# Up projection of a hybrid decoder layer: 16 of 22 tile pairs with seven products, in runs of three and four

## The reference, cut to what matters

```python
h2 = _rmsnorm(x, g_ffn)
f = jnp.einsum("btd,df->btf", h2, w_up)
f_gate, f_up = jnp.split(f, [D_FF], axis=-1)
f_conv, new_f = _causal_dwconv(f_gate, buf_f, conv_f_w)
x = x + jnp.einsum("btf,fd->btd", jax.nn.silu(f_conv) * f_up, w_down)
```

## Time and profile before

| | us |
|---|---|
| median of 3 runs | 856.12 (856.05 to 856.14) |
| the profiled execution: its own time | 856.21 |
| its span, first to last instruction | 854.2 |
| PE busy | 840.2 (98%) |
| DVE busy | 665.6 (78%) |
| ACT busy | 407.7 (48%) |
| mean granted clock of TensorE | 0.999 |

### The profile page before, as it was taken

How to read it: one execution, slowest core, us unless ns; L and a number is a source line. 1 busy time by engine, 2 the same in 40 slices (tenths; PEclk the granted TensorE clock), 3 DMA queues, 4 the chain that set the end, 5 groups by cost and what they waited for, 6 DMA issues and landing times.

```text
span 854.2 us, 18315 instructions
## 1 busy us (share of the span) xinstructions
PE 840.2 (98%) x6948; PEld 835.8 (98%) x6948; DVE 665.6 (78%) x983; ACT 407.7 (48%) x733; POOL 128.9 (15%) x98
## 2 busy tenths in 40 slices
PE   8999999999999999999999989999999999999996
PEld 7999999999999999999999979999999999999996
DVE  4899998999999965766579898888888888544343
ACT  7753646364342244762245655454454457332232
POOL 2283837475000000000012200000000000000000
PEclk9999999999999999999999999999999999999999
DMA  9423233432432333218632123333333334353323
GB/s 258 125 85 113 76 98 98 134 100 87 126 104 76 99 110 99 76 49 159 161 100 74 50 81 101 97 94 100 102 97 101 107 92 129 93 133 98 95 75 113
DMA packets 189160, 88.92 MB, mean 104 GB/s; under 512 B 34758, under 2 KB 187644, under 8 KB 189076
## 3 DMA queue, kind: packets, MB, share of 16 engines
q1 hardware_dynamic: 186225, 86.29, 36.0%
q10 hardware_dynamic: 2875, 1.82, 0.8%
HBM read 83.79 MB, written 3.51 MB: 102 GB/s over the span
## 4 chain that ended last, share of the span: by engine, by line
PE 91%; DVE 5%; issue 1%; ACT 1%; DMA 0%; DVEq 0%; SPq 0%; ACTq 0%
PE psum L1715 44%; PE psum L1721 22%; PE psum L1891 8%; PE psum L1919 6%; PE psum L1896 4%; PE psum L1924 3%; PE psum L2032 1%; DVE w_lo L1364 1%; DVE tmp L1474 1%; PE psum L2041 1%; PE psum L1693 1%; PE psum L1758 1%; PE psum L1756 1%; DMA v<-in_x_prompt 0%; PE psum L1765 0%
## 5 line engine op out<-in xcount | busy, mean ns | idle before, releaser
L1715 PE MATMUL psum<-act,w_hi 128*128 128x260 f32 x2600 | 341.1, 282 | 0.0
L1715 PEld LDWEIGHTS psum<-act,w_hi 128*128 128x128 f32 x2600 | 323.0, 188 | 0.0
L1069 DVE TENSOR_TENSOR w_lo<-raw,w_hi 128x1024 fp32r<-128x1024 f32 (+2 forms) x110 | 129.9, 1183 | 77.2 <-ACT w_hi L544 76.7
L1721 PE MATMUL psum<-act,w_lo 128*128 128x260 f32 x1300 | 185.1, 282 | 0.0
L1721 PEld LDWEIGHTS psum<-act,w_lo 128*128 128x128 f32 x1300 | 168.1, 188 | 0.0
L544 ACT ACTIVATE w_hi<-raw 128x1024 fp32r<-128x1024 f32 (+2 forms) x110 | 107.1, 976 | 88.2 <-PE psum L1721 85.7
L512 POOL TENSOR_TENSOR gate_a<-gate_a,prods 128x512 f32<-128x512 f32 x72 | 110.1, 1529 | 79.6 <-ACT prods L629 71.2
L1891 PE MATMUL psum<-act,w_hi 128*128 128x260 f32 x448 | 71.3, 283 | 3.0 <-ACT tmp L891 2.7
L1364 DVE TENSOR_TENSOR w_lo<-raw,w_hi 128x1024 fp32r<-128x1024 f32 x44 | 53.6, 1222 | 24.2 <-ACT w_hi L815 24.2
L1919 PE MATMUL psum<-mid,w_hi 128*128 128x260 f32 x512 | 68.1, 283 | 0.0
L1146 DVE SCALAR_TENSOR_TENSOR psum<-u,cst,psum 128x512 f32<-128x512 f32 x96 | 66.8, 746 | 0.0
(11 more groups left out here) (208 smaller groups left out, 999.6 us busy)
## 6 DMA issues: line engine op xcount, KB each, us to landing
raw<-in_w_in SPq DMA_DIRECT2D x56, 512.0 KB, 3.7
raw<-in_w_up SPq DMA_DIRECT2D x44, 512.0 KB, 3.8
raw<-in_w_down SPq DMA_DIRECT2D x16, 384.0 KB, 3.9
raw<-in_w_down SPq DMA_DIRECT2D x16, 320.0 KB, 3.2
v<-in_x_prompt SPq DMA_DIRECT2D x8, 512.0 KB, 6.3
raw<-in_w_b_out SPq DMA_DIRECT2D x8, 512.0 KB, 3.7
raw<-in_w_a_out SPq DMA_DIRECT2D x8, 512.0 KB, 5.1
raw<-in_w_o SPq DMA_DIRECT2D x8, 512.0 KB, 4.3
```

Source lines behind the costliest of these rows:

```text
L1069: ve.tensor_tensor(w_lo[:, slot, 0:k, :], raw[:, s, 0:k, :], w_hi[:, slot, 0:k, :], ALU.subtract).then_inc(lo_done, 1)
L1715: pe.matmul(a[:, h, :], w_hi[:, s, j, :], rhs(k, part)[:, h * H:(h + 1) * H], start=start and part == 0, stop=False)
L1721: last = pe.matmul(a[:, h, :], w_lo[:, s, j, :], rhs(k, 0)[:, h * H:(h + 1) * H], start=False, stop=stop)
```

## The change

The plain steps are now 0, 4, 8, 13, 17 and 21: six, and 16 steps have seven products, in runs of three (1 to 3, 5 to 7, 14 to 16, 18 to 20) and one of four (9 to 12). The chain's bank comes from a table: in a run of three banks 0, 2, 3, in a run of four banks 0, 1, 2, 3. Since banks 0 and 1 are also those of the plain gate product, two waits come in: P1 of a step whose bank is 0 or 1 waits for `cx_set` of the last plain step (DVE's `plain_gate` has read the gate banks), and a plain gate product waits for `prod_done` of the last step that used them. On ACT `silu(n - 1)` moves behind `up_5(n)` in steps that follow another step with seven, and in step 1; in the other first steps of a run it stays ahead of `up_v`. On DVE `weight_sum_4(n + 1)` moves ahead of `up_22(n)`. `turn_root` goes with the third plain step, now step 8.

```diff
-    PLAIN = tuple(range(0, FT, 3))
+    PLAIN = (0, 4, 8, 13, 17, 21)
...
+        IN_RUN = [n - max(m for m in PLAIN if m <= n) - 1 for n in range(FT)]
+        RUN = [next((m for m in PLAIN if m > n), FT) - max(m for m in PLAIN if m <= n) - 1 for n in range(FT)]
+        BANK_X = [((0, 2, 3) if RUN[n] == 3 else (0, 1, 2, 3))[IN_RUN[n]] if SEVEN[n] else None for n in range(FT)]
...
         def bank_x(n):
-            return psum[:, 2 if TURN[n] else 3, 0:H]
+            return psum[:, BANK_X[n], 0:H]
...
         def last_x(n):
-            return max((m for m in range(n) if SEVEN[m] and TURN[m] == TURN[n]), default=None)
+            return max((m for m in range(n) if BANK_X[m] == BANK_X[n]), default=None)
+
+        def last_in_gate_banks(n):
+            return max(m for m in range(n) if BANK_X[m] in (0, 1))
...
                 hi_open(n + 1)
-                if FOLLOWS[n]:
-                    up_v(n)
+                if not FOLLOWS[n] and n > 1:
                     silu(n - 1)
-                else:
+                up_v(n)
+                up_5(n)
+                if FOLLOWS[n] or n == 1:
                     silu(n - 1)
-                    up_v(n)
-                up_5(n)
...
-                up_22(n)
                 if SEVEN[n + 1]:
                     weight_sum_4(n + 1)
+                up_22(n)
...
                     pe.wait_ge(cx_set, PLAIN[PLAIN.index(n) - 1] + 1)
+                    pe.wait_ge(prod_done, START + 2 * KT + last_in_gate_banks(n) + 1)
                     plain(n, "gate", gate_banks, 1, at_4=lambda: fourth(n - 1))
...
                 if last_x(n) is not None:
                     pe.wait_ge(prod_done, START + 2 * KT + last_x(n) + 1)
+                if BANK_X[n] in (0, 1):
+                    pe.wait_ge(cx_set, max(m for m in PLAIN if m < n) + 1)
                 product("P1", n)
```

More of the change, by code:

```diff
@@ L310, in build @@
         assert PLAIN[0] == 0 and PLAIN[-1] == FT - 1 and SEVEN[1]
+        IN_RUN = [n - max(m for m in PLAIN if m <= n) - 1 for n in range(FT)]
+        RUN = [next((m for m in PLAIN if m > n), FT) - max(m for m in PLAIN if m <= n) - 1 for n in range(FT)]
+        BANK_X = [((0, 2, 3) if RUN[n] == 3 else (0, 1, 2, 3))[IN_RUN[n]] if SEVEN[n] else None for n in range(FT)]
+        assert all(RUN[n] in (3, 4) for n in range(FT) if SEVEN[n])
         def bank_x(n):
-            return psum[:, 2 if TURN[n] else 3, 0:H]
+            return psum[:, BANK_X[n], 0:H]
         def banks_zy(n):
```

## The result

The changed kernel takes 863.87 us, the median of 4 runs (863.71 to 864.04), against 856.12 before (4 runs, 856.05 to 856.14): a ratio of 1.0091, 95% interval 1.0076 to 1.0106. It is 7.75 us slower; 8.0 were forecast. The profiled execution took 863.88 us with a span of 861.8, so the 2.0 us around the span are unchanged. The down projection starts at 727.44 us, where it started at 719.88 before. The first matmul of the up projection starts at 478.44, where it was 478.57. So this stage is 7.69 us longer and what lies ahead of it 0.13 shorter, and nothing behind it changed. PE's busy time fell by 0.4 us and DVE's rose by 9.3.

The account below looks back on a forecast made before the run. PE, 91% of the chain, was taken to bound the kernel through its work and waits. Terms -3.0 + 1.8 + 9.75 + 1.7 - 2.0 = +8.2, taken as +8.0 on 856.21, gave 864.2 us; range 862.4 to 866.6.

Parts of the forecast that it names:

- The matmuls saved: On PE, two plain steps become steps with seven products, 11.57 to 10.06 us each: 3.0 us down.
- P1 of step 1: P1 waits for `cx_set` and starts 5.2 us late; after waits that shrink, step 3 begins 1.8 us later: 1.8 up.
- The clock: Forecast: clock stays at 1.00 behind step 1's wait. Rival (30%): it falls in the 5.2 us idle, +9.1, 865.3 us.
- Middle steps: Steps 2, 6, 10, 11, 15, 19: DVE needs 12.0 us, PE 10.06, so P4 waits for `up_22`; with step 3, 9.75 up.
- the lead of each run: How far `up_22`'s result is ahead of P4 at a run's start: 1.0 us, between 0.9 and 1.5.
- P1 of a run's first step: P1 waits for `plain_gate`: 1.5 us at step 9 behind `turn_root`, 0.2 at step 5; together 1.7 up.
- Waits that go: `silu` behind the copies frees P3 in the last step of a run: 0.7, 0.9 and four times 0.1, 2.0 down.
- The price of a later `silu`: On ACT, moving `silu` behind the copies was put at nothing, as DVE has other work ahead of the product needing it.
- The likeliest case: The forecast as worked out, +8.0 us to 864.2, without a clock fall: 60%, 862.4 to 865.
- not slower: Rival (3%): DVE keeps up in middle steps as its 1.34 us wait for ACT shrinks; -0.5, 855.7 us.

Follow-up runs that it names:

- The experiment that keeps PE busy: The changed kernel with 42 matmuls without use into free bank 2 ahead of P1 of step 1, whose wait stays: 862.43 us.
- the experiment with another bank: The changed kernel with banks 2, 0, 3 in the first run, so that P1 of step 1 has a free bank: 860.15 us.
- orders alone: The kernel before with only the change's two order edits, `silu` on ACT and `weight_sum_4` on DVE; runs of two and old banks stay: 853.05 us.
- POOL: The kernel with banks 2, 0, 3 first and earlier weight sums, plus the third weight-sum pass on POOL and plain steps 0, 3, 9, 15, 21: 855.08 us.
- both repairs: The changed kernel with banks 2, 0, 3 in the first run and `weight_sums(n + 1)` ahead of `lo_3(n)` in middle steps: 853.50 us.
- another bank behind `turn_root`: The changed kernel with banks 2, 0, 1, 3 in the run of four (steps 9 to 12): 863.19 us.

## Why the prediction was right

The sign, the size and the places were right. By the steps of the sum:

- *The matmuls saved*, 3.0 down: 6924 matmuls on the page, where 6948 stood before: 24 fewer.
- *P1 of step 1*, 1.8 up without the clock. The start at 495.84 and the idle time of 5.2 were met to 0.07 us (495.91, 5.19). With the clock's fall step 3 began at 517.48 and not at 516.4, so that the term came to 2.85. The experiment that keeps PE busy puts 1.4 us on the fall and the restart. One reason given was wrong: the wait of 2.4 for `up_v` was to go because `silu(0)` no longer stands ahead of it. With the same order and P1 on time (the experiment with another bank) 1.92 of it is left; in the changed kernel it is gone because PE comes 5.2 us late itself.
- *The clock*: this is where the forecast chose wrongly. It gave the fall 30% because 2.4 us of idle had done nothing before. That was one profiled execution, and three later kernels fell at the same place after 1.92. That the earlier trace rows are matmuls at the lower level is not in the profile of the kernel before, whose window from 11 to 12 us reads 1.00; the changed kernel's trace shows this pace beside a clock of 0.50. The rival's own numbers held: P1's products 0.217 apart, P1 some 1.2 later where 1.1 was said, 1.1 more on the sum. The rule of the Trainium skill named there (TensorE: Matmul & The Clock Gate, section "Why this matters for your kernels"), that idle gaps between bursts of matmuls drop TensorE to its lower clock, agrees with this trace: 5.19 us idle, and 0.50.
- *Middle steps*, 9.75 up: the mis-sized term. All six waits came, in the order of size forecast (2.0, 1.8, 1.05, 2.0, 1.05, 1.05), but at 1.84, 1.55, 0.75, 1.72, 0.75 and 0.74; with 0.65 in step 3 the term is 8.0. The step that was off is "a middle step takes DVE 12.0 us": it takes 11.80, and the bound put beside it let it only grow, to 12.2. The 12.0 added `weight_sum_4` at its full 0.60. But in the earlier trace rows `up_22` starts 0.83 behind the product on whose semaphore it waits, and in the changed kernel 0.60 behind a pass that it need not wait for. Two tenths of that 0.6 were already being lost. It counts twice, in the loop and in the lead of each run.
- *P1 of a run's first step*, 1.7 up: counted by starts, 1.58 at step 9 and 0.14 at step 5, as forecast. But as the price of `turn_root` the 1.5 is too high: without that wait the kernel gains only 0.7.
- *Waits that go*, 2.0 down: no wait for `up_5` is left. Put back in its old place, `silu` costs 4.2. The price of a later `silu` was put at nothing, and nothing shows.

The sum is then -3.0 + 2.85 + 8.0 + 1.7 - 2.0 = +7.55, and 7.56 were measured at the start of the down projection. The forecast of +8.0 had the middle steps, step 3 included, 1.75 too high, and it left out the 1.05 of the clock. So 864.2 is near to 863.87 partly by luck, because two errors cancel. The likeliest case with the right loop and no fall would have read 862.4 to 862.7 (864.2 less 1.75, the upper end without the rounding of 8.2 to 8.0), and the experiment without a fall measured 862.43, though it also spared PE the restart.

The rival "not slower" had its mechanism half right: the 1.35 us that DVE waits for ACT do not shrink when DVE is late, as was argued against it, but they can be filled by a change of order, and then a middle step is short enough and the loss is gone.

## What to carry to other kernels

When work is added to an engine's step, first find the wait that this engine already has in the step, and put the added work there; the same three passes cost 7.0 us more behind the wait than ahead of it, where one wait for `up_22` of 0.2 was left. Take a change apart into its edits before judging it: here the two orders were worth 3.0 us and the longer runs cost 10.8, of which a bank and a place in a list gave back 10.4. And a wait in front of a stretch that another engine bounds is not free time to be won in full: half of the one at step 9 came back a step later.

## What the runs showed of the hardware that was not expected

The granted clock does not follow from the length of the last wait alone. In the profile of the kernel before, PE waited 2.45 us ahead of P7 of step 1 and the clock stayed at 1.00. In three other kernels (another bank, orders alone, POOL) it waited 1.92 us at the same place and the clock fell to 1.2 GHz, each time when PE was already at work again; in the one with both repairs it waited 1.91 us and the clock stayed. After 5.2 us of idle it fell in every profile, between 492 and 493 in the changed kernel and at 496.0, as P1 began, in the one with another bank behind `turn_root`. The kernel with the orders alone and then the one with both repairs, windows with PEclk ahead of the last two columns:

```profile
500.00:505.00 5.00, 5.00 (x31) 5.00 (x31) 4.86 (x9) 1.83 (x3) 0.00 (x0) 0.66 0.36 105
```

```profile
500.00:505.00 5.00, 4.34 (x36) 4.14 (x35) 4.86 (x9) 1.77 (x3) 0.00 (x0) 1.00 0.36 105
```

Executions of one kernel differ in it too: of the kernel with the orders alone one has the fall and two, with a mean of 0.999, can't. What a fall costs was different at the two places: 1.4 us, restart included, where ACT and DVE wait for the product next, and nothing that can be seen where PE waits for them next.

DVE's pass of 1.22 us took 2.22 beside a POOL pass that reads SBUF, so a pass of 0.60 handed to POOL cost DVE more than it freed: 10.85 us per middle step in place of 10.35.
